# The recurrent branch of a fused two-block kernel: decay bias added on VectorE, decay and gate products interleaved, both running sums in one product

## The chip, the cores and the metric

The kernel runs as one program on one core of a Trainium2 chip. The time is the device time of one execution in microseconds (us), and the kernel before took 2842.14 us (median of three runs, 2840.62 to 2842.34). The engines are called by the profile's short names: PE (TensorE matmul), PEld (its weight loads), DVE (VectorE), ACT (ScalarE), POOL (GpSimd) and SP (SyncE, which issues the weight transfers).

## The reference, cut to what matters

The whole program is a first block (spatial gating, dilated attention, two mixtures of experts) followed by a second block of two layers. Each of these two layers is a feed-forward part, a mixer of three branches (retention, sparse attention, recurrence), and another feed-forward part. The change is in the recurrent branch alone, so it runs twice in an execution.

```python
def rwkv7_time_mix(p, mu, w0, w2, a0, a2, g2, k_k, k_a, r_k, ln_w, ln_b):
    r, k, v, w_lr, a_lr, g_lr = split_cols(token_shift(p, mu), RWKV_SIZES)
    log_decay = -jax.nn.softplus(-(w0 + jnp.tanh(w_lr) @ w2).astype(f32)) - 0.5
    decay = jnp.exp(-jnp.exp(log_decay))
    a = jax.nn.sigmoid((a0 + a_lr @ a2).astype(f32))
    g = jax.nn.sigmoid(g_lr) @ g2
    kk = heads(k * k_k)
    kk = kk / jnp.maximum(jnp.sqrt(jnp.sum(kk * kk, axis=-1, keepdims=True)), 1e-12)
    k_h = heads(k) * (1.0 + (a_h - 1.0) * k_a...)
    ...  # a scan over 256 tokens with decay, k_h, kk and a; then a group norm and the gate g
```

Here exp(log_decay) is exp(-0.5) times sigmoid(w0 + tanh(w_lr) w2). The kernel does the scan in chunks of 64 tokens, and needs for that the running sum of this sigmoid over the tokens of a chunk, once with the token itself (inclusive) and once without it (strict), and exponentials of both.

## The kernel before, in words

There are 256 tokens, held as two tiles of 128 (`T` = 2), and 512 channels of the branch, held as four tiles of 128. Every engine has its own program, and all meet at numbered pieces of PSUM: piece n lies in bank n modulo 4 (`BANKS`). PE fills a piece (`pe.take()`, wait on `s_free`, then the products with `s_full` at the end), and the engine that reads it frees the bank (`s_free`). Each engine's program counts every piece, and passes with `skip` over those that are others' work. So PE can't start piece n before piece n - 4 has been read, and the engine that reads a piece does it when its own program gets there. There is no planner; the order is as written, on each engine.

Around the change, PE's order in `pe_rwkv` (line 2845) is this:

- the channel products of the branch (`pe_chan`), then `pe_merge_sparse(0)`: a gate product and a product of the sparse branch, one piece each
- `pe_headsum_of_tokens(TMP)`: eight products with two output columns each, one piece. DVE reads it in `v_rates_of_tokens` (lines 2828 to 2834)
- for each token tile, the decay product (`LORA[0:64]` with the upper 64 rows of `LR`) and a product with one row, ones times `W0R`, that adds the bias w0 in the same piece (lines 2876 and 2877)
- four products of `LORA[64:128]` for a, two pieces (line 2882), and four of `G2` for the gate g, two pieces (line 2889)
- the running sums: `LWT` times the table `cumulate`, whose first 128 columns make the strict and the other 128 the inclusive sum; the inclusive ones first (`m` = 1), two pieces each, 16 products in all (line 2902)
- `pe_to_heads(RSS)`: 32 small products that spread the reciprocal norms of kk over the channels, two pieces, then `pe_merge_sparse(1)` and so on.

ACT reads the decay pieces with a sigmoid (line 3068), the a pieces with a sigmoid and the bias a0 (3073), copies the g pieces (3079), takes the square root of the head norms (line 827, in `s_root`), and then does the exponentials of the sums (3084, 3085, 3089). The square root and the exponential each need a load of ACT's function table. DVE, after `v_merge_sparse(0)`, makes the low part of a split weight block (`v_ahead(34)`, line 2038), which waits for ACT's high part of the same block (`s_ahead(34)`, line 2030), which waits for the block's transfer; then comes `v_rates_of_tokens` (line 2832), and the next thing is the reciprocal of the roots (2838). Block 34 is one of the weight blocks that SP loads into a ring of five slots. `s_params` (line 2305) issues the transfers of the branch's small weights, w0's at line 2310, at the start of the layer's mixer.

## Time and profile before

| | |
|---|---|
| device time, median of three runs | 2842.14 us (2840.62 to 2842.34) |
| span of the profiled execution, first to last instruction | 2833.1 us |
| PE busy | 2648.3 us (93%) |
| DVE busy | 1269.9 us (45%) |
| ACT busy | 838.0 us (30%) |
| mean granted clock of TensorE, as a share of full speed | 0.980 |
| this stretch in layer 1 of the second block | about 1656 to 1684 us |
| this stretch in layer 2 | about 2454 to 2481 us |

The profile gives one execution by its span, 2833.1 us. A run's time also holds what lies ahead of the first instruction and behind the last one: 9.0 us against the median. A busy share of 93% for PE is an average over the whole program. What a change in one stretch is worth must be read in the stretch: which engine is waited for there, and how fast TensorE's clock runs in it.

### The profile page before, as it was taken

To read this page: it belongs to the slowest core of one execution; us is meant where nothing else is said; L and a number is where in the kernel's file an instruction comes from. 1 tells how busy PE (TensorE), PEld (TensorE's weight loads), DVE (VectorE), ACT (ScalarE), POOL (GpSimd) and SP (SyncE) were. 2 spreads that over 40 slices of the span, in tenths; PEclk is the share of its full clock that TensorE was granted. 3 is DMA by queue.
4 is the path that set the end of the run, shared out by engine and by line. 5 is a ranking of instruction groups with operands and counts; after the bars stand their busy time and mean duration, and the time that the engine had idled before them with its cause. 6 is when DMAs were issued, how large, how long until landed. Compare 5 with 4: busy or idle time off the path is not lost.

```text
span 2833.1 us, 46156 instructions
## 1 busy us (share of the span) xinstructions
PE 2648.3 (93%) x19543; PEld 2036.8 (72%) x19543; DVE 1269.9 (45%) x1869; ACT 838.0 (30%) x1039; POOL 0.2 (0%) x4
## 2 busy tenths in 40 slices
PE   8899888879899888879999999999999999999998
PEld 8743433348543333369999889999899998899998
DVE  5610110046411000055657756655655667666555
ACT  4300000025210000033343432443433444423433
POOL 0000000000000000000000000000000000000000
PEclk9999999999999999999999999999999999999999
DMA  8689999972799999955563431445555544323553
GB/s 269 256 358 425 426 425 426 425 267 90 311 401 425 425 425 425 426 170 182 196 218 122 133 119 62 135 164 179 179 179 190 186 152 134 105 76 102 167 179 134
DMA packets 286235, 684.65 MB, mean 242 GB/s; under 512 B 11962, under 2 KB 217586, under 8 KB 236660
## 3 DMA queue, kind: packets, MB, share of 16 engines
q1 hardware_dynamic: 282792, 671.27, 63.2%
q10 hardware_dynamic: 3276, 10.93, 1.0%
q8 instruction: 132, 2.16, 0.3%
q14 instruction: 35, 0.29, 0.0%
HBM read 681.11 MB, written 1.05 MB: 241 GB/s over the span
## 4 chain that ended last, share of the span: by engine, by line
PE 71%; DMA 20%; DVE 5%; ACT 2%; issue 1%; DVEq 1%; SPq 0%; ACTq 0%; POOLq 0%
PE psum L419 69%; DMA weight_ring<-in_w_gate 14%; DMA weight_ring<-in_w_up 3%; DMA weight_ring<-in_w_down 2%; PE psum L427 1%; DVE weight_ring_parts L2038 1%; ACT weight_ring_parts L2030 1%; DVEq L552 1%; DVE arena L3230 0%; DMA h_tok<-in_mem 0%; SPq L1893 0%; DVE arena L3256 0%; DVE arena L1809 0%; DMA weight_ring<-in_w_in 0%; DVE arena_parts L2127 0%
## 5 line engine op out<-in xcount | busy, mean ns | idle before, releaser
L419 PE MATMUL psum<-weight_ring_parts,arena_parts 128*128 128x256 f32 (+1 forms) x2992 | 671.5, 317 | 4.9 <-DVE arena_parts L2131 1.9
L2038 DVE TENSOR_TENSOR weight_ring_parts<-weight_ring,weight_ring_parts 128x2048 fp32r<-128x2048 f32 x217 | 496.6, 2291 | 347.1 <-ACT weight_ring_parts L2030 341.1
L419 PE MATMUL psum<-x_chan_parts,weight_ring_parts 128*128 128x256 f32 x3200 | 611.5, 282 | 13.1 <-DVE arena_parts L2127 7.9
L2030 ACT ACTIVATE weight_ring_parts<-weight_ring 128x2048 fp32r<-128x2048 f32 x217 | 414.9, 1913 | 483.3 <-POOLq L532 347.4
L419 PE MATMUL psum<-weight_ring,arena 128*64 128x512 f32 (+1 forms) x2112 | 474.8, 582 | 73.5 <-DMA weight_ring<-in_w_gate 38.9
L419 PEld LDWEIGHTS psum<-weight_ring_parts,arena_parts 128*128 128x128 f32 x2992 | 501.5, 191 | 41.4 <-DVE arena_parts L2131 2.1
L419 PEld LDWEIGHTS psum<-x_chan_parts,weight_ring_parts 128*128 128x128 f32 x3200 | 508.5, 190 | 18.5 <-issue 13.2
L419 PE MATMUL psum<-arena 64*64 64x64 f32 (+7 forms) x4616 | 492.6, 335 | 29.5 <-DVE arena L1809 15.8
L419 PEld LDWEIGHTS psum<-weight_ring,arena 128*64 128x64 f32 (+1 forms) x2112 | 179.3, 140 | 361.1 <-issue 358.2
L419 PEld LDWEIGHTS psum<-arena 64*64 64x64 f32 (+3 forms) x4616 | 261.3, 141 | 237.3 <-issue 210.9
L419 PE MATMUL psum<-weight_ring_parts,x_chan_parts 128*128 128x256 f32 x2336 | 427.8, 285 | 1.6 <-DVE arena_parts L2127 1.6
L419 PE MATMUL psum<-arena_parts,weight_ring_parts 128*128 128x256 f32 x1536 | 419.2, 283 | 0.0
L419 PEld LDWEIGHTS psum<-weight_ring_parts,x_chan_parts 128*128 128x128 f32 x2336 | 360.8, 190 | 9.2 <-issue 7.5
L419 PEld LDWEIGHTS psum<-arena_parts,weight_ring_parts 128*128 128x128 f32 x1536 | 285.2, 190 | 1.3
L1825 DVE TENSOR_TENSOR arena<-arena,psum 128x512 f32<-128x512 f32 x32 | 22.0, 688 | 520.8 <-PE psum L419 519.5
L1809 DVE COPY arena<-psum 128x512 f32<-128x512 f32 x48 | 33.2, 692 | 296.8 <-PE psum L419 262.4
L1671 ACT ACTIVATE arena<-psum 128x512 f32<-128x512 f32 x32 | 19.1, 597 | 484.4 <-PE psum L419 484.4
L1664 ACT ACTIVATE arena<-psum 128x512 f32<-128x512 f32 (+1 forms) x80 | 34.3, 467 | 371.3 <-PE psum L419 334.5
L2038 DVE TENSOR_TENSOR weight_ring_parts<-weight_ring,h_tok_parts 128x2048 fp32r<-128x2048 f32 x32 | 73.3, 2292 | 64.7 <-ACT h_tok_parts L2030 63.9
L419 PE MATMUL psum<-arena_parts,h_tok_parts 128*128 128x256 f32 x320 | 90.0, 281 | 0.0
L419 PE MATMUL psum<-x_chan_parts,h_tok_parts 128*128 128x256 f32 x320 | 89.6, 280 | 0.0
L2030 ACT ACTIVATE h_tok_parts<-weight_ring 128x2048 fp32r<-128x2048 f32 x32 | 61.1, 1911 | 71.5 <-POOLq L532 34.2
(322 smaller groups left out, 1742.9 us busy)
## 6 DMA issues: line engine op xcount, KB each, us to landing
weight_ring<-in_w_gate SPq DMA_DIRECT2D x92, 1024.0 KB, 23.2
weight_ring<-in_w_up SPq DMA_DIRECT2D x92, 1024.0 KB, 22.9
weight_ring<-in_w_in SPq DMA_DIRECT2D x70, 1024.0 KB, 5.2
arena<-in_w_down SPq DMA_DIRECT2D x64, 1024.0 KB, 22.5
weight_ring<-in_w_down SPq DMA_DIRECT2D x64, 1024.0 KB, 23.2
weight_ring<-in_ffa_w_in SPq DMA_DIRECT2D x44, 1024.0 KB, 7.2
weight_ring<-in_ffb_w_in SPq DMA_DIRECT2D x44, 1024.0 KB, 5.6
arena<-in_w_gate SPq DMA_DIRECT2D x36, 1024.0 KB, 18.5
```

The lines of the kernel that those rows point to most:

```text
L419: return nc.tensor.matmul(*args, **kw)
L427: last = nc.tensor.transpose(ps[0:cols, b, lo:lo + rows], src, ident[0:rows, 0:rows])
L552: self.e.drain()
L1664: nc.scalar.activation(dst, ps[:, b, 0:dst.shape[1]], ACT.Copy).then_inc(s_free[b], 1)
L1671: nc.scalar.activation(SILU[:, half, :], ps[:, b, :], ACT.Silu).then_inc(s_free[b], 1)
L1809: nc.vector.tensor_copy(dst, ps[:, b, :]).then_inc(s_free[b], 1)
L1825: nc.vector.tensor_tensor(HG[:, half * 512:(half + 1) * 512], SILU[:, half, :], ps[:, b, :], ALU.mult).then_inc(s_free[b], 1)
L2030: nc.scalar.activation(HIGH[buf], ring[:, sl, :], ACT.Copy).then_inc(s_hi, 1)
L2038: nc.vector.tensor_tensor(ring_parts[:, sl, :], ring[:, sl, :], f32(HIGH[buf]), ALU.subtract).then_inc(s_split, 1)
```

## The change

There are three edits, and one that follows from them.

1. The bias w0 is no longer a product. It is loaded as 128 equal rows (`W0B`) where it was one row (`W0R`), DVE adds it to the decay piece on the way into `LWT` in SBUF, and ACT takes the sigmoid there, in place, once DVE has signalled it.
2. The decay product of a token tile, which uses the upper 64 rows of the array, is followed at once by two of the four products of a, which use the lower 64 rows.
3. The strict and the inclusive sum of a channel and token tile are one product with 256 moving columns. A piece then holds both sums of one channel tile, so that ACT takes its exponentials per channel tile, 256 elements each.
4. PE waits for two signals from ACT ahead of the running sums, where it waited for the two banks to be read. The square root needs no wait of its own.

```diff
-        W0R = sb("decay_bias_row", [1, 512])
+        W0B = sb("decay_bias_rows", [P, 512])
...
-            s.e.dma_start(W0R[0:1, :], a["rwkv_w0_2"][bass.ds(l, 1), :]).then_inc(s_load["w0"], 16)
+            s.e.dma_start(W0B[:, :], a["rwkv_w0_2"][l].partition_broadcast(P)).then_inc(s_load["w0"], 16)
...
-                pe.mm(ps[:, b, :], LR[0:64, 0, t * P:(t + 1) * P], LORA[0:64, :], start=True, stop=False)
-                pe.mm(ps[:, b, :], ones2[0:1, :], W0R[0:1, :], start=False, stop=True).then_inc(s_full[b], 1)
-            for c in range(0, 4, 2):
+                pe.mm(ps[:, b, :], LR[0:64, 0, t * P:(t + 1) * P], LORA[0:64, :], start=True, stop=True).then_inc(s_full[b], 1)
                 b = pe.take()
                 pe.e.wait_ge(s_free[b], pe.emptied())
                 for j in range(2):
-                    last = pe.mm(ps[:, b, j * SEQ:(j + 1) * SEQ], LORA[64:128, (c + j) * P:(c + j + 1) * P],
+                    c = 2 * t + j
+                    last = pe.mm(ps[:, b, j * SEQ:(j + 1) * SEQ], LORA[64:128, c * P:(c + 1) * P],
                                  LR[64:128, 0, :], start=True, stop=True)
...
-            for m in (1, 0):
-                for c in range(0, 4, 2):
-                    b = pe.take()
-                    pe.e.wait_ge(s_free[b], pe.emptied())
-                    for j in range(2):
-                        for t in range(T):
-                            last = pe.mm(ps[:, b, j * SEQ + t * P:j * SEQ + (t + 1) * P],
-                                         LWT[:, t, (c + j) * P:(c + j + 1) * P], cumulate[:, m * P:(m + 1) * P],
-                                         start=True, stop=True)
-                    last.then_inc(s_full[b], 1)
+            pe.e.wait_ge(s_a2p, pe.c["a2p"].next(T))
+            for c in range(4):
+                b = pe.take()
+                pe.e.wait_ge(s_free[b], pe.emptied())
+                for t in range(T):
+                    last = pe.mm(ps[:, b, t * 2 * P:(t + 1) * 2 * P], LWT[:, t, c * P:(c + 1) * P], cumulate,
+                                 start=True, stop=True)
+                last.then_inc(s_full[b], 1)
...
             for t in range(T):
-                b = s.take()
-                s.e.wait_ge(s_full[b], s.filled())
-                nc.scalar.activation(LWT[:, t, :], ps[:, b, :], ACT.Sigmoid).then_inc(s_free[b], 1)
-            for c in range(0, 4, 2):
+                s.skip()
+
+                s.e.wait_ge(s_v2a, s.c["v2a"].next(2 if t == 0 else 1))
+                nc.scalar.activation(LWT[:, t, :], LWT[:, t, :], ACT.Sigmoid).then_inc(s_a2p, 1)
...
-            s_root(RSS[:, :, :])
+            nc.scalar.activation(RSS[:, :, :], RSS[:, :, :], ACT.Sqrt).then_inc(s_a2v, 1)
...
+            for c in range(4):
                 b = s.take()
                 s.e.wait_ge(s_full[b], s.filled())
+                sums = ps[:, b, :].rearrange("p (t m n) -> p m t n", t=T, m=2)
+                nc.scalar.activation(by_token_tile(PI, c), sums[:, 1], ACT.Exp, scale=-DECAY)
+                nc.scalar.activation(by_token_tile(IPI, c), sums[:, 1], ACT.Exp, scale=DECAY)
+                nc.scalar.activation(by_token_tile(PEX, c), sums[:, 0], ACT.Exp, scale=-DECAY).then_inc(s_free[b], 1)
...
             v_rates_of_tokens(1.0, 1e-24, ALU.mult, ALU.max)
-            rates = v.pieces.n + 2
-            v.skip(10)
+            v.e.wait_ge(s_load["w0"], v.c["l_w0"].next())
+            rates = v.pieces.n + 1
+            for t in range(T):
+                b = v.take()
+                v.e.wait_ge(s_full[b], v.filled())
+                nc.vector.tensor_tensor(LWT[:, t, :], ps[:, b, :], W0B[:, :], ALU.add).then_inc(s_free[b], 1)
+                v.sync()
+                nc.vector.nop().then_inc(s_v2a, 1)
+                v.skip()
+            v.skip(6)
```

On PE, behind the products of the head norms (`tables,arena 128x2`), the difference reads as follows. `norm_gain_bias` holds `LORA` and `G2`, `decay_bias_row` is `W0R`, and `piece_free2_two` is the bank of the head norms.

```order
 L419 MATMUL psum<-tables,arena 128x2 x7
-L419 MATMUL psum<-norm_gain_bias,arena 128x512 [waits scalar_to_tensor_two,piece_free3_two,loaded_w0,loaded_lora]
-L419 MATMUL psum<-decay_bias_row,tables 128x512
-L419 MATMUL psum<-norm_gain_bias,arena 128x512 [waits piece_free0_two]
-L419 MATMUL psum<-decay_bias_row,tables 128x512
-L419 MATMUL psum<-arena,norm_gain_bias 128x256 [waits piece_free1_two]
+L419 MATMUL psum<-norm_gain_bias,arena 128x512 [waits piece_free3_two,scalar_to_tensor_two,loaded_lora]
+L419 MATMUL psum<-arena,norm_gain_bias 128x256 [waits piece_free0_two]
 L419 MATMUL psum<-arena,norm_gain_bias 128x256
+L419 MATMUL psum<-norm_gain_bias,arena 128x512 [waits piece_free1_two]
 L419 MATMUL psum<-arena,norm_gain_bias 128x256 [waits piece_free2_two]
 L419 MATMUL psum<-arena,norm_gain_bias 128x256
```

The two one-row products are gone, the second decay product stands behind the first two products of a, and the wait for bank 2 stays where it was, with the third product of a, now with two products fewer ahead of it.

On ACT, at the same place, before:

```order
L2030 ACTIVATE weight_ring_parts<-weight_ring 128x2048 [waits slots_used_two,slot_loaded4_two]
L3068 ACTIVATE arena<-psum 128x512 [waits piece_full3_two]
L3068 ACTIVATE arena<-psum 128x512 [waits piece_full0_two]
L3073 ACTIVATE arena<-psum,small 128x256 [waits piece_full1_two]
L3073 ACTIVATE arena<-psum,small 128x256
L3073 ACTIVATE arena<-psum,small 128x256 [waits piece_full2_two]
L3073 ACTIVATE arena<-psum,small 128x256
L3079 ACTIVATE arena<-psum 128x512 [waits piece_full3_two]
L3079 ACTIVATE arena<-psum 128x512 [waits piece_full0_two]
L827 ACT_TABLE_LOAD
L827 ACTIVATE small<-small 128x16 [waits vector_to_scalar_two]
L3084 ACT_TABLE_LOAD
```

and ACT now, where line 3062 is the decay's sigmoid, 3067 that of a, 3073 the copy of g, 3074 the root, and 3083 the first exponential:

```order
L2030 ACTIVATE weight_ring_parts<-weight_ring 128x2048 [waits slots_used_two,slot_loaded4_two]
L3062 ACTIVATE arena<-arena 128x512 [waits vector_to_scalar_two]
L3067 ACTIVATE arena<-psum,small 128x256 [waits piece_full0_two]
L3067 ACTIVATE arena<-psum,small 128x256
L3062 ACTIVATE arena<-arena 128x512 [waits vector_to_scalar_two]
L3067 ACTIVATE arena<-psum,small 128x256 [waits piece_full2_two]
L3067 ACTIVATE arena<-psum,small 128x256
L3073 ACTIVATE arena<-psum 128x512 [waits piece_full3_two]
L3073 ACTIVATE arena<-psum 128x512 [waits piece_full0_two]
L3074 ACT_TABLE_LOAD
L3074 ACTIVATE small<-small 128x16
L3083 ACT_TABLE_LOAD
```

Both decay sigmoids now wait for DVE and not for PE, and the second stands between the two pairs for a; the copies, the root and the two table loads keep their order.

## Rows read from the trace of the kernel before

**Rows 1.** The page: its first line, and GB/s moved in 40 equal slices of the span.
```profile
span 2833.1 us, 46156 instructions
...
GB/s 269 256 358 425 426 425 426 425 267 90 311 401 425 425 425 425 426 170 182 196 218 122 133 119 62 135 164 179 179 179 190 186 152 134 105 76 102 167 179 134
```

**Rows 2.** Chain that ended last, 1640 to 1740: start us, length us, what.
```profile
1680.95 31.41 PE psum L419 x228
```

**Rows 3.** Timeline, layer 1: start us, length us, engine, line, what [idle before <-releaser].
```profile
1656.85 3.62 PE L419 MATMUL psum<-weight_ring,arena 128*128 128x256 f32 x16
...
1660.50 0.69 DVE L2387 TENSOR_TENSOR arena<-arena,psum 128x512 f32<-128x512 f32 x1 [2.56 <-PE psum L419]
...
1662.07 1.12 PE L419 MATMUL psum<-norm_gain_bias,arena 64*128 64x512 f32 x2
...
1663.12 1.71 PE L419 MATMUL psum<-decay_bias_row,tables 1*128 1x512 f32 x2
1663.46 1.91 ACT L2030 ACTIVATE weight_ring_parts<-weight_ring 128x2048 fp32r<-128x2048 f32 x1 [5.82 <-DMA weight_ring<-in_w_in]
...
1664.76 2.07 PE L419 MATMUL psum<-norm_gain_bias,arena 64*128 64x512 f32 x2
...
1665.40 2.29 DVE L2038 TENSOR_TENSOR weight_ring_parts<-weight_ring,weight_ring_parts 128x2048 fp32r<-128x2048 f32 x1 [3.43 <-ACT weight_ring_parts L2030]
...
1666.76 2.07 PE L419 MATMUL psum<-decay_bias_row,tables 1*128 1x512 f32 x2
1667.61 0.17 DVE L2832 TENSOR_SCALAR small<-psum 128x16 f32<-128x16 f32 x1
...
1668.76 7.49 PE L419 MATMUL psum<-arena,norm_gain_bias 64*128 64x256 f32 x16
...
1670.87 0.84 ACT L3073 ACTIVATE arena<-psum,small 128x256 f32<-128x256 f32 x2 [1.41 <-PE psum L419]
1672.47 3.06 PEld L419 LDWEIGHTS psum<-arena,norm_gain_bias 128*128 128x128 f32 x8 [0.65 <-issue]
...
1676.04 4.29 PE L419 MATMUL psum<-tables,arena 128*128 128x128 f32 x32
1676.29 0.60 ACT L3079 ACTIVATE arena<-psum 128x512 f32<-128x512 f32 x1 [1.11 <-PE psum L419]
...
1679.72 0.60 ACT L3084 ACTIVATE arena<-psum 128x512 f32<-128x512 f32 x1
...
1680.22 0.59 ACT L3085 ACTIVATE arena<-psum 128x512 f32<-128x512 f32 x1
...
1680.95 1.98 PE L419 MATMUL psum<-tables,small 128*64 128x128 f32 x32 [0.62 <-ACT arena L3085]
...
1682.86 0.50 PE L419 MATMUL psum<-weight_ring_parts,x_chan_parts 128*128 128x256 f32 x2
```

**Rows 4.** Timeline, layer 2, the same stretch.
```profile
2464.66 0.17 DVE L2832 TENSOR_SCALAR small<-psum 128x16 f32<-128x16 f32 x1
...
2472.96 3.73 PE L419 MATMUL psum<-tables,arena 128*128 128x128 f32 x32
...
2476.60 0.60 ACT L3084 ACTIVATE arena<-psum 128x512 f32<-128x512 f32 x1
...
2479.74 0.51 PE L419 MATMUL psum<-weight_ring_parts,x_chan_parts 128*128 128x256 f32 x2
```

**Rows 5.** Busy time by stretch; PEclk, after the engines, is the granted clock.
```profile
1663.00:1664.00 1.00, 1.00 (x3) 0.29 (x2) 0.00 (x0) 0.54 (x1) 0.00 (x0) 0.76 0.00 0
...
1676.00:1678.00 2.00, 2.00 (x14) 1.96 (x13) 0.00 (x0) 1.70 (x2) 0.00 (x0) 0.70 0.00 0
...
2476.00:2478.00 2.00, 0.87 (x11) 0.70 (x11) 1.93 (x4) 1.99 (x4) 0.00 (x0) 1.00 0.00 0
```

**Rows 6.** The instructions of line 3073: duration ns min/median/max, first and last start.
```profile
L3073 ACT ACTIVATE arena<-psum,small x8: 466/470/473, 1670.9 to 2470.3; 128x256 f32<-128x256 f32 x8
```

**Rows 7.** DMA issues: queue, count, KB each, median us to landing.
```profile
norm_gain_bias<-in_rwkv_g ACTq DMA_DIRECT2D x2, 256.0 KB, 9.1
```

More of the change, by code:

```diff
@@ L2869, in pe_rwkv @@
             pe.e.wait_ge(s_load["lora"], pe.c["l_lora"].next(3))
-            pe.e.wait_ge(s_load["w0"], pe.c["l_w0"].next())
             pe.e.wait_ge(s_a2p, pe.c["a2p"].next())
@@ L2891, in pe_rwkv @@
                 last.then_inc(s_full[b], 1)
-            pe.e.wait_ge(s_free[(pe.pieces.n - 6) % BANKS], pe.read_out(pe.pieces.n - 6))
-            pe.e.wait_ge(s_free[(pe.pieces.n - 5) % BANKS], pe.read_out(pe.pieces.n - 5))
-            for m in (1, 0):
-                for c in range(0, 4, 2):
-                    b = pe.take()
-                    pe.e.wait_ge(s_free[b], pe.emptied())
-                    for j in range(2):
-                        for t in range(T):
-                            last = pe.mm(ps[:, b, j * SEQ + t * P:j * SEQ + (t + 1) * P],
-                                         LWT[:, t, (c + j) * P:(c + j + 1) * P], cumulate[:, m * P:(m + 1) * P],
-                                         start=True, stop=True)
-                    last.then_inc(s_full[b], 1)
+            pe.e.wait_ge(s_a2p, pe.c["a2p"].next(T))
[6 more added lines that the diff above has]
+                last.then_inc(s_full[b], 1)
             pe_to_heads(RSS)
@@ L3072, in s_rwkv @@
                 for j in range(2):
-                    last = nc.scalar.activation(WA[:, c + j, :], ps[:, b, j * SEQ:(j + 1) * SEQ], ACT.Sigmoid,
-                                                bias=pv("rwkv_a0")[:, c + j:c + j + 1])
+                    c = 2 * t + j
+                    last = nc.scalar.activation(WA[:, c, :], ps[:, b, j * SEQ:(j + 1) * SEQ], ACT.Sigmoid,
+                                                bias=pv("rwkv_a0")[:, c:c + 1])
                 last.then_inc(s_free[b], 1)
@@ L3079, in s_rwkv, with by_token_tile @@
                 nc.scalar.activation(flat(WG[:, c:c + 2, :]), ps[:, b, :], ACT.Copy).then_inc(s_free[b], 1)
-            s_root(RSS[:, :, :])
-            for c in range(0, 4, 2):
+            nc.scalar.activation(RSS[:, :, :], RSS[:, :, :], ACT.Sqrt).then_inc(s_a2v, 1)
+            def by_token_tile(x, c):
+                return x[:, c, :].rearrange("p (t n) -> p t n", t=T)
+            for c in range(4):
                 b = s.take()
                 s.e.wait_ge(s_full[b], s.filled())
-                nc.scalar.activation(flat(PI[:, c:c + 2, :]), ps[:, b, :], ACT.Exp, scale=-DECAY)
-                nc.scalar.activation(flat(IPI[:, c:c + 2, :]), ps[:, b, :], ACT.Exp, scale=DECAY).then_inc(s_free[b], 1)
-            for c in range(0, 4, 2):
-                b = s.take()
-                s.e.wait_ge(s_full[b], s.filled())
-                nc.scalar.activation(flat(PEX[:, c:c + 2, :]), ps[:, b, :], ACT.Exp, scale=-DECAY).then_inc(s_free[b], 1)
+                sums = ps[:, b, :].rearrange("p (t m n) -> p m t n", t=T, m=2)
+                nc.scalar.activation(by_token_tile(PI, c), sums[:, 1], ACT.Exp, scale=-DECAY)
+                nc.scalar.activation(by_token_tile(IPI, c), sums[:, 1], ACT.Exp, scale=DECAY)
+                nc.scalar.activation(by_token_tile(PEX, c), sums[:, 0], ACT.Exp, scale=-DECAY).then_inc(s_free[b], 1)
             s.skip(2)
@@ L3171, in v_rwkv @@
             v_rates_of_tokens(1.0, 1e-24, ALU.mult, ALU.max)
-            rates = v.pieces.n + 2
-            v.skip(10)
+            v.e.wait_ge(s_load["w0"], v.c["l_w0"].next())
[8 more added lines that the diff above has]
+            v.skip(6)
             v_reciprocal_of_rates()
-            for n in (rates, rates + 1):
+            for n in (rates, rates + 2):
                 v.e.wait_ge(s_free[n % BANKS], v.read_out(n))
```

## Prediction

> **What bounds the kernel now.** I started with the page. The span is 2833.1 us [rows 1] and PE is busy for 93% of it, which says only that PE is usually the bound. Then I read the chain that ended last, in order of time, around this stretch of layer 1. It has one unbroken piece of PE from 1680.95 on, 31.41 us long [rows 2], and the pieces just before it are on ACT. The timeline shows why. PE does the running sums from 1676.04, but what comes next, the spreading of the norms at 1680.95, waits 0.62 us for ACT's exponential of line 3085, which frees its bank [rows 3]. ACT is late since its work is serial behind PE: the last copy of g starts at 1676.29, 0.25 us behind PE's last gate product (PE's next work starts at 1676.04), and then come the copy (0.60), two table loads and the root, so that the first exponential starts at 1679.72. So 3.43 us lie between the start of the last copy and the first exponential, and 3.68 between the end of PE's gate products and it. In layer 2 the same distance is 2476.60 - 2472.96 = 3.64 [rows 4].
>
> What the reader is to see: in this stretch the end is set by PE's products up to the last gate product, plus ACT's fixed 3.7 us, and not by the running sums. And PE's products are dear here. The first decay product took 1.05 us to the next start (1662.07 to 1663.12), the second 2.00 (1664.76 to 1666.76) [rows 3]. The windows say why: the granted clock averages 0.76 in 1663 to 1664, so it falls to its lower level of 1.2 GHz about half way, and averages 0.70 in 1676 to 1678, so it comes back about 1677.2 [rows 5]. Four gate products at the low level took 1676.04 - 1672.47 = 3.57 us (0.89 each), four products of a 1672.47 - 1668.76 = 3.71 (0.93 each); at full clock eight products of 256 columns (16 records, two for each) took 3.62 us, 0.45 each at most [rows 3].
>
> There is a third chain, hidden now. DVE reads the head norms only at 1667.61, behind the low part of weight block 34 at 1665.40, behind ACT's high part at 1663.46, which waited for the block's transfer [rows 3]. Call the end of that read V: 1667.61 + 0.17 = 1667.78 in layer 1, and 2464.66 + 0.17 = 2464.83 in layer 2 [rows 3, 4]. It frees bank 2, for which the third product of a waits. Before, PE reached that product about 1668.76 + 1.86 = 1670.6, 2.8 us later than V, so nobody waited.
>
> **The change part by part.** The time is the span plus 9.0 us for what lies around it (2842.14 - 2833.1), and I take the change of the span as the change of the time.
>
> *Bias products removed.* From start to next start they took 1.64 us (1663.12 to 1664.76) and 2.00 us (1666.76 to 1668.76), so 3.64 in layer 1 [rows 3]. Taken alone that would be the gain, and some 7 us in both layers. It can't all arrive: PE now runs into the wait for V.
>
> *Decay and a in alternating halves.* The first decay product, two of a, and the second decay product need between 1.9 us (if the halves run beside each other) and 3.0 us (2 x 1.05 and 2 x 0.45, one after the other at full clock). PE starts them at 1662.07 and is through by 1665.1 at the latest at full clock, and by about 1666.5 if the clock falls at 1663.5 as before. V is at 1667.78. So whatever the halves give, PE then idles for 1.3 to 3.8 us. I cost the interleaving at zero: its cover is the wait for V. If block 34 were early, it would be worth up to 1.1 us a layer.
>
> *PE behind V.* I take the low clock, since it had fallen before with PE busy and now PE idles as well. Two products of a cost 1.86, four gate products 3.57 (their banks are freed by DVE's first add at about V + 0.8 and by ACT's first pair at about V + 2.3, both earlier than PE needs them). With 0.05 to start, PE is through at V + 5.48: 1673.26 in layer 1, where it was 1676.04, and 2470.31 in layer 2, where it was 2472.96. So -2.78 and -2.65.
>
> *ACT and the DVE adds.* Each add is a 128x512 DVE operation from PSUM like the one at 1660.50, 0.69 us [rows 3]; with hand-over about 0.1. The first sigmoid of the decay can start at V + 0.9, the second at V + 2.2. With 0.5 to 0.6 for each (the copy of 512 elements took 0.60), and 0.84 or less for each pair of a (the row at 1670.87), ACT is through with a at V + 3.5 to V + 3.8, while PE's first gate piece is ready at about V + 3.7 and its second at V + 5.5. At the low clock ACT waits for PE, and the sigmoids cost nothing. At full clock they would be the bound, see the rivals.
>
> *Fixed tail.* Copy, two table loads and root are unchanged: first exponential at PE's end + 3.68. So 1676.94 and 2473.95 (with 3.64).
>
> *Running sums.* Eight products of 256 columns where there were 16 of 128, the same columns. Bounds: 3.6 us at full clock (8 x 0.45), 7.1 at the low one (8 x 0.89). From V + 5.5 they end between V + 9.1 and V + 12.6. The first bank is released by the exponentials at V + 10.5. So they are covered if the clock comes back within some 4 us of their start. It came back 4.7 us behind the start of the gate products in layer 1 (1672.47 to 1677.2), hence I take V + 6.7 and the sums end near V + 9.7: covered.
>
> *Narrower exponentials.* This speaks against the change. Those of 512 elements follow each other at 0.50 us (1679.72 to 1680.22); two of 256 took 0.84 together [rows 3] with 0.47 for one [rows 6], so they follow at 0.37. Twelve cost 11 x 0.37 + 0.47 = 4.5 us where six cost 5 x 0.50 + 0.60 = 3.1. What counts is when PE can go on. The merge product needed the bank freed by the fifth one, and before it started 1682.86 - 1679.72 = 3.14 behind the first exponential, being held up by the spreading products. Now it needs the ninth: 8 x 0.37 + 0.47 + 0.14 = 3.57. That is +0.43 a layer. Bounds: 0 (spreading alone decides) and +0.85 (spacing 0.42).
> The Trainium skill, page "VectorE: DVE Perf Modes", section on the TRN2 errata, says that an ACT or DVE operation pays a fixed cost per instruction, so that many small tiles pay it many times, and gives ScalarE 172 cycles plus one per element for PSUM sources. By that estimate twelve narrow ones cost 12 x 0.36 = 4.3 us and six wide ones 6 x 0.57 = 3.4, a rise of 0.9 where the rows give 1.4. The rows decide, and the sum stands.
>
> *The wider transfer.* w0 is now 256 KB where it was 2 KB, the size of g2's block, which lands in 9.1 us [rows 7]. It is issued at the start of the mixer and needed only behind V, after the retention and the sparse branch. It could hold up the weight blocks beside it by its own length, between 0 and 0.6 us (254 KB at the page's highest rate of 426 GB/s [rows 1]); I take 0, since only the queue's order is changed and the blocks are loaded ahead of their use.
>
> *Sum.* -2.78 + 0.43 = -2.35 in layer 1, -2.65 + 0.43 = -2.22 in layer 2, together -4.6 us. Behind 1682.86 PE is dense for 30 us [rows 2], and the loads that feed it are released by PE itself, so the gain should reach the end. 2842.14 - 4.6 = 2837.5, a span of about 2828.5.
>
> **The rivals.**
>
> *A. ACT bound, full clock: more gain.* If TensorE's clock is back while PE does a and g, ACT's own row from V is the bound: first decay sigmoid V + 0.9, 0.5, pair 0.74, 0.5, pair 0.74, copies 0.50 + 0.60, so V + 4.5, and 2.83 for tables and root: first exponential at V + 7.3. That is 1675.1 and 2472.1, or -4.6 and -4.5; less 0.43 each, -8.2 in all: 2833.9. For it: bias and half-empty products, which stood in the stretch where the clock fell, are fewer. Against: PE idles ahead of V. A mixture, the clock returning during the gate products, lies between.
>
> *B. Running sums are the bound: the gain nearly vanishes.* If the clock stays low until they are done (V + 12.6), spreading starts at V + 12.6 where it was V + 13.2, and itself takes 1.9 to 3.8. Between -0.6 and +1.3 a layer: about 2842.5, and 2840.5 if one layer only is so. Against: the clock came back 4.7 us into such products.
>
> *C. Slower: the clock falls a second time.* The change leaves PE idle for about 0.8 us (V + 9.7 to V + 10.5) ahead of the 32 small spreading products. If the clock then falls and stays low into the merge products, each us of it costs up to half. It decides against the change beyond some 4.6 us low in each layer. A low stretch as long as before (1663.5 to 1677.2, 13.7 us) would cost 6.8 a layer, 13.7 - 4.6 = +9.1: 2851; a short one of 6 us in each layer 6 - 4.6 = +1.4: 2843.6. Against: in layer 2 PE was busy for 0.87 of 2 us in 2476 to 2478 at a clock of 1.00, and full clock went on [rows 5].
> The Trainium skill, page "TensorE: Matmul & The Clock Gate", names gaps between bursts of products as what sends the clock back to half; by it both the wait for V and this gap are a risk, while the rows show one such gap without a fall.
>
> *D. The transfer of w0 delays the entry of the layer.* At most 0.6 each, +1.2 on the forecast: 2838.7.
>
> **How the numbers follow.** Forecast, including the clock returning a little earlier during the gate products (up to 1 us a layer more): 0.56. A: 0.12. B: 0.18. C: 0.07. D: 0.07. A measurement of this kernel tells 0.2%, or 5.7 us, from no change, so the line lies at 2836.5. Faster gets A and a third of the forecast's share: 0.30. Slower by over 0.2% (2847.8) is only the long form of C: 0.05; the rest, 0.65, is within. The range goes from A's time to just above B's: 2833.9 to 2842.3.
>
> **What would show it.** Right: DVE's read of the head norms stays near 1667.6, the first exponential of layer 1 at about 1677, the merge product at about 1680.5; PE idle ahead of the third product of a with DVE line 2832 as what it waited for; the releaser of the spreading products is ACT's third exponential; the clock low from the decay products to the first running sums. Wrong: if the first exponential lies before 1676, the clock was back (A); if PE is busy right up to the spreading products, the sums were the bound (B); a clock below 1.00 in the merge products is C. The forecast fails as a whole if block 34 lands at another time, as V is the origin of everything.

## The result, and the profile after

The changed kernel took 2830.40 us (median of 20 runs, 2824.58 to 2839.78). The kernel before, run beside it, took 2838.03 (20 runs, 2830.68 to 2842.34). The ratio is 0.9978, 95% interval 0.9969 to 0.9987, which on 2838.03 is -6.2 us (-8.8 to -3.7); the quotient of the two medians, 0.9973, lies in that interval. So the change makes the kernel faster by about 0.2%. The forecast of -4.6 us lies in that interval. The forecast time, 2837.5, doesn't fit, and 2830.4 lies below the range that ended at 2833.9.

The profiled execution of the changed kernel has this span:

```profile
span 2836.5 us, 46096 instructions
```

Its time was 2838.36 us, near the upper end of its 20 runs, and only 1.9 us lie around its span. It can't be set against the span of before, 2833.1 [rows 1], to read the gain: these two executions differ by more than the change. Between 2540 and 2610 us, in code that the change doesn't touch, the two compare as follows, first before, then after (columns as in [rows 5], the clock is the third number from the end):

```profile
2540.00:2610.00 70.00, 68.13 (x1140) 63.91 (x1136) 42.45 (x63) 22.45 (x28) 0.00 (x0) 1.00 0.23 78
```

```profile
2540.00:2610.00 70.00, 68.43 (x947) 63.94 (x943) 35.53 (x54) 20.19 (x22) 0.00 (x0) 0.85 0.23 73
```

TensorE is busy alike, at a clock of 0.85 where it was 1.00. By an estimate from these rows that alone costs about 70 x 0.15 = 10 us. It isn't the change's doing: in the second profile of the changed kernel (see the last experiment) the same stretch has a clock of 1.00. The runs differ in the same way: of the changed kernel's, the shortest had a mean clock of 0.985 (2824.58 us) and the longest 0.976 (2839.78). I therefore compare the changed stretch by its own length, from the first two-column product of the head norms to the first product of the following merge, and the whole by runs.

The chain that ended last, in layer 1, after the change (start us, length us, what):

```profile
1658.35 6.37 DMA weight_ring<-in_w_in
...
1664.75 1.92 ACT weight_ring_parts L2030
...
1666.69 2.29 DVE weight_ring_parts L2038
...
1669.12 5.80 PE psum L419 x12
...
1674.94 0.60 ACT arena L3073
...
1675.55 1.28 ACT L3074
...
1678.38 0.38 ACT arena L3083
...
1679.46 20.70 PE psum L419 x157
```

Ahead of the products of a, the chain now goes through weight block 34: its transfer, ACT's high part, DVE's low part. That chain was hidden before, behind the bias products. The timeline of layer 1 after, which answers to [rows 3]:

```profile
1661.56 1.84 PE L419 MATMUL psum<-tables,arena 128*128 128x2 f32 x16
...
1663.33 0.69 PE L419 MATMUL psum<-norm_gain_bias,arena 64*128 64x512 f32 x1
1663.34 0.70 PE L419 MATMUL psum<-arena,norm_gain_bias 64*128 64x256 f32 x2
...
1664.30 1.02 PE L419 MATMUL psum<-norm_gain_bias,arena 64*128 64x512 f32 x2
...
1668.90 0.17 DVE L2832 TENSOR_SCALAR small<-psum 128x16 f32<-128x16 f32 x1
1669.12 5.78 PE L419 MATMUL psum<-arena,norm_gain_bias 64*128 64x256 f32 x12 [3.80 <-DVE small L2832]
...
1674.69 4.11 PE L419 MATMUL psum<-tables,arena 128*128 128x256 f32 x16
...
1678.38 0.38 ACT L3083 ACTIVATE arena<-psum 128x256 f32<-128x256 f32 x1
...
1678.66 0.38 ACT L3084 ACTIVATE arena<-psum 128x256 f32<-128x256 f32 x1
1678.92 0.39 ACT L3085 ACTIVATE arena<-psum 128x256 f32<-128x256 f32 x1
...
1679.46 1.97 PE L419 MATMUL psum<-tables,small 128*64 128x128 f32 x32 [0.65 <-ACT arena L3085]
...
1681.35 0.50 PE L419 MATMUL psum<-weight_ring_parts,x_chan_parts 128*128 128x256 f32 x2
```

PE is through with its first work at 1665.3 and idles 3.80 us until DVE has read the head norms (V, 1669.07). The sums start at 1674.69 = V + 5.62, the first exponential 3.69 later, and the merge product 2.97 behind that. In layer 2 the wait is 2.58 us:

```profile
2463.48 4.70 PE L419 MATMUL psum<-arena,norm_gain_bias 64*128 64x256 f32 x12 [2.58 <-DVE small L2832]
```

The clock in layer 1 after, which answers to [rows 5], and the last three rows are in layer 2:

```profile
1664.00:1666.00 2.00, 1.31 (x7) 0.25 (x3) 0.00 (x0) 1.25 (x1) 0.00 (x0) 1.00 0.01 3
1666.00:1668.00 2.00, 0.00 (x0) 0.00 (x0) 1.31 (x1) 0.66 (x1) 0.00 (x0) 1.00 0.00 0
1668.00:1670.00 2.00, 0.88 (x2) 0.79 (x3) 1.76 (x3) 0.00 (x0) 0.00 (x0) 0.71 0.00 0
1670.00:1672.00 2.00, 2.00 (x5) 1.17 (x5) 0.69 (x1) 1.95 (x5) 0.00 (x0) 0.50 0.00 0
...
1674.00:1676.00 2.00, 2.00 (x7) 1.61 (x6) 0.00 (x0) 1.04 (x2) 0.00 (x0) 0.58 0.00 0
1676.00:1678.00 2.00, 2.00 (x11) 1.74 (x11) 0.90 (x4) 1.97 (x3) 0.00 (x0) 1.00 0.00 0
1678.00:1680.00 2.00, 1.35 (x14) 0.95 (x14) 1.84 (x4) 1.99 (x8) 0.00 (x0) 1.00 0.00 0
...
2462.00:2464.00 2.00, 0.52 (x2) 0.48 (x3) 1.80 (x3) 0.00 (x0) 0.00 (x0) 1.00 0.00 0
2464.00:2466.00 2.00, 2.00 (x6) 1.16 (x5) 1.01 (x2) 1.60 (x4) 0.00 (x0) 0.54 0.00 0
2466.00:2468.00 2.00, 2.00 (x7) 1.60 (x6) 0.00 (x0) 1.56 (x4) 0.00 (x0) 0.61 0.00 0
```

Before, TensorE's clock fell at about 1663.5, with PE busy on decay and bias products. After, in layer 1, it stays at full through these products and through two microseconds without any, and falls at about 1668.8, near the end of the idle time. In layer 2 it is still at full when PE goes on at 2463.48, and falls at about 2464.2, so the fall comes with the wait for V, but not always inside it. It is at 1.2 GHz for about 7 us in layer 1 (before: 13.7) and 3.4 in layer 2 (before: 10.2), from windows of 1 us.

The stage in us from its start, layer 1 / layer 2, in all kernels whose cause is argued below ("late" is block 34's split moved behind the exponentials, see the experiments):

| kernel | V | sums start | first exponential | merge product | change of both stages |
|---|---|---|---|---|---|
| before | 7.48 / 6.53 | 15.74 / 14.66 | 19.42 / 18.30 | 22.56 / 21.44 | |
| changed | 7.51 / 6.28 | 13.13 / 10.86 | 16.82 / 14.50 | 19.79 / 17.48 | -6.7 |
| changed, second profile | 7.42 / 6.33 | 12.95 / 10.61 | 16.63 / 14.29 | 19.61 / 17.26 | -7.1 |
| bias on VectorE only | 7.62 / 6.47 | 13.25 / 11.05 | 16.93 / 14.69 | 20.07 / 17.84 | -6.1 |
| no alternation | 7.58 / 6.00 | 13.20 / 10.20 | 16.88 / 13.88 | 19.86 / 16.86 | -7.3 |
| sums joined only | 7.60 / 6.16 | 14.66 / 14.63 | 18.30 / 18.27 | 21.28 / 21.25 | -1.5 |
| before, late | 2.05 / 2.05 | 14.67 / 15.40 | 18.30 / 19.08 | 21.45 / 22.22 | -0.3 |
| the same, bias full height | 2.05 / 2.05 | 15.72 / 15.37 | 19.40 / 19.06 | 22.54 / 22.20 | +0.7 |
| the same, bias behind a | 2.04 / 2.05 | 7.44 / 7.45 | 11.59 / 11.60 | 14.73 / 14.74 | -14.5 |
| the same, no bias | 2.05 / 2.05 | 5.54 / 5.54 | 9.66 / 9.66 | 12.80 / 12.80 | -18.4 |
| changed, late | 2.05 / 2.05 | 6.16 / 6.15 | 10.20 / 10.19 | 13.17 / 13.17 | -17.7 |
| changed, late, no alternation | 2.05 / 2.05 | 6.11 / 6.10 | 10.51 / 10.50 | 13.49 / 13.48 | -17.0 |
| changed, late, g copied by VectorE | 2.05 / 2.05 | 6.15 / 6.15 | 9.22 / 9.22 | 12.20 / 12.20 | -19.6 |

### The profile page after: what moved, and what is told of

Its sections match the earlier page's. It is cut to its first block, busy times and chain, and to the rows that moved or that the text cites. A ratio compares the mean times of both kernels' runs of the same rounds, so it can differ in the third digit from the quotient of the medians.

```text
span 2836.5 us, 46096 instructions
## 1 busy us (share of the span) xinstructions
PE 2646.5 (93%) x19503; PEld 2041.3 (72%) x19503; DVE 1272.4 (45%) x1873; ACT 838.5 (30%) x1051; POOL 0.2 (0%) x4
## 3 DMA queue, kind: packets, MB, share of 16 engines
HBM read 681.63 MB, written 1.05 MB: 241 GB/s over the span
## 4 chain that ended last, share of the span: by engine, by line
PE 70%; DMA 20%; DVE 5%; ACT 2%; issue 1%; DVEq 1%; SPq 0%; ACTq 0%; POOLq 0%
PE psum L419 69%; DMA weight_ring<-in_w_gate 14%; DMA weight_ring<-in_w_up 3%; DMA weight_ring<-in_w_down 2%; DVE weight_ring_parts L2038 1%; PE psum L427 1%; ACT weight_ring_parts L2030 1%; DVEq L552 1%; DMA weight_ring<-in_w_in 0%; DVE arena L3234 0%; DMA weight_ring<-in_w_in_a 0%; DMA h_tok<-in_mem 0%; SPq L1893 0%; DVE arena L3260 0%; PE psum L686 0%
```

## The experiments

**Is the wait for V the new bound?** Block 34's split (`s_ahead(34)` and `v_ahead(34)`) moves from ahead of the decay work to behind the exponentials; nothing else of the changed kernel does.

```diff
             s_merge_sparse(0)
-            s_ahead(34)
...
             s.skip(2)
+            s_ahead(34)
             s_merge_sparse(1)
...
             v_merge_sparse(0)
-            v_ahead(34)
             v_rates_of_tokens(1.0, 1e-24, ALU.mult, ALU.max)
...
+            v_ahead(34)
             v_merge_sparse(1)
```

> The changed kernel, with the split of weight block 34 moved on ACT and DVE from ahead of the head norms' read to behind the exponentials, so that V (the end of DVE's read of the head norms) no longer waits for that block's transfer. Stage length = from the start of PE's head-norm products (128x2) to the start of the first product of the next merge; it was 22.6 and 21.4 us before and is 19.8 and 17.5 in the changed kernel. Theory (V is the bound behind the change): V falls to about 0.3 us behind the head-norm products, PE does not wait ahead of the third product of a, the bound becomes ACT's own row (V + 7.3 to the first exponential, 3.0 more to the merge), stage length 12.5 to 15 us in both layers, 5 to 12 us less in all than the changed kernel, ratio to before 0.993 to 0.996. Rival (the gain came from fewer product columns at the low clock, V is only a bystander): stage length falls by under 1 us against the changed kernel, ratio 0.998. Rival 2: the gain is given back in the later merge, whose product waits for block 34's low part: PE idle there by the 4 us that were saved.

Measured: 2819.07 us (6 runs), ratio 0.9930 (0.9914 to 0.9945) to the kernel before at 2836.98, that is -19.9 us; the two stages are 17.7 shorter. PE no longer waits for V, and the clock stays at full:

```profile
1662.16 0.59 PE L419 MATMUL psum<-norm_gain_bias,arena 64*128 64x512 f32 x1
1662.17 1.70 PE L419 MATMUL psum<-arena,norm_gain_bias 64*128 64x256 f32 x6
1664.18 1.13 PE L419 MATMUL psum<-arena,norm_gain_bias 128*128 128x256 f32 x4 [0.31 <-ACT arena L3066]
1665.15 3.62 PE L419 MATMUL psum<-tables,arena 128*128 128x256 f32 x16
1670.27 1.97 PE L419 MATMUL psum<-tables,small 128*64 128x128 f32 x32 [1.50 <-ACT arena L3084]
```

```profile
1659.00:1672.00 13.00, 11.19 (x85) 9.34 (x83) 6.86 (x12) 9.17 (x22) 0.00 (x0) 1.00 0.09 29
```

The wait for V was the bound in the changed kernel, and the clock fell with it: without the wait it doesn't fall. With it gone ACT's row is the bound: PE waits for ACT's exponentials for 1.50 us.

**Is the late block alone worth it?** The same move in the kernel before.

> The kernel before with only block 34's split moved behind the exponentials. Theory: before the change PE reached the third product of a 2.8 us behind V in layer 1, so V was not the bound there: stage length stays at 22.6 and 21.4 us within 1 us, ratio 1.000 (0.999 to 1.001). Rival (the block was the bound all along and the change itself did little): stage length falls by 2 us or more, ratio 0.998 or less.

Measured: 2837.68 us (12 runs), ratio 0.9996 (0.9980 to 1.0012); the stages change by -1.1 and +0.8. Nothing, since PE never waited for V there. The -17.7 are a joint effect: the change brings the wait for V into the open, and only then is moving block 34 worth something. The timeline of this kernel shows the dear products still there, with V already past:

```profile
1662.63 1.12 PE L419 MATMUL psum<-norm_gain_bias,arena 64*128 64x512 f32 x2
1663.69 1.12 PE L419 MATMUL psum<-decay_bias_row,tables 1*128 1x512 f32 x2
1664.74 1.79 PE L419 MATMUL psum<-norm_gain_bias,arena 64*128 64x512 f32 x2
1666.46 2.07 PE L419 MATMUL psum<-decay_bias_row,tables 1*128 1x512 f32 x2
1668.45 3.78 PE L419 MATMUL psum<-arena,norm_gain_bias 64*128 64x256 f32 x8
```

**What is the alternation worth?** The changed kernel with both decay products ahead of the four products of a (on all engines), first as it is, then with block 34 late.

```diff
             for t in range(T):
                 b = pe.take()
                 pe.e.wait_ge(s_free[b], pe.emptied())
                 pe.mm(ps[:, b, :], LR[0:64, 0, t * P:(t + 1) * P], LORA[0:64, :], ...)
+            for t in range(T):
                 b = pe.take()
```

> The changed kernel with only the alternation undone: both decay products, then the four products of a; the rest as changed. Theory: V covers it, stage length as in the changed kernel, 19.8 and 17.5 us within the 1.5 us that the clock's return can move it, PE idle ahead of the third product of a 0.9 us shorter, ratio to before 0.998. Rival (alternation is what made the gain or held the clock): stage length 21 us or more, clock low for 10 us or more in the stretch as before.

> As the kernel with block 34 late, but both decay products first and then the four products of a (one half of the array after the other). Here the wait for V no longer covers it. Theory (interleaving was worth nothing in the change because V covered it): now PE needs up to 0.9 us more for the six products at full clock, but ACT is the bound, so the stage is 0 to 0.9 us longer per layer than with alternation. Rival (the halves beside each other are what keeps the clock up): the granted clock falls to its low level in this stretch and the stage is 2 us or more longer.

Measured: 2825.90 us (7 runs), ratio 0.9963 (0.9949 to 0.9977), and late 2817.62 (6 runs), 0.9930 (0.9913 to 0.9947). The first is no slower than the changed kernel, its stages are even 0.6 us shorter, little more than the 0.4 by which the changed kernel's two profiles differ. I had expected PE's idle time ahead of the third product of a to be 0.9 us shorter, and it wasn't: 3.88 us where it was 3.80, behind 1.99 us of work in either order. With block 34 late the alternation is worth 0.3 us a layer, and that on ACT's side, since PE starts the sums at 6.11 without and 6.16 with it. The reason is in the timeline without alternation. Its program has decay, decay, a, a, a, a, each float32 product recorded as two:

```profile
1662.94 0.69 PE L419 MATMUL psum<-norm_gain_bias,arena 64*128 64x512 f32 x1
1662.96 0.70 PE L419 MATMUL psum<-arena,norm_gain_bias 64*128 64x256 f32 x2
1663.48 0.59 PE L419 MATMUL psum<-norm_gain_bias,arena 64*128 64x512 f32 x1
1663.49 0.59 PE L419 MATMUL psum<-arena,norm_gain_bias 64*128 64x256 f32 x2
1663.90 0.59 PE L419 MATMUL psum<-norm_gain_bias,arena 64*128 64x512 f32 x1
```

The first products of a start 0.02 us behind the first decay product and ahead of the second: two halves of the array run side by side although the program doesn't alternate.

**The bias on VectorE alone, and the joined sums alone.** The first has the new adds with the old order and the old 16 sums, the second the kernel before with only the 8 wide sums and the 12 narrow exponentials.

> The kernel before with edit 1 alone: w0 is added by DVE and the sigmoid is taken in place; both decay products come first, then the four of a; the running sums are 16 products of 128 columns and six exponentials of 512 elements, as before. Stage length (start of the 128x2 head-norm products to the first product of the next merge) was 22.6 and 21.4 us before and 19.8 and 17.5 in the changed kernel. Theory (edit 1 carries the gain, down to the wait for V): 20.0 us in layer 1 and 17 to 18.5 in layer 2, the changed kernel's plus 0.2 for the tail, ratio 0.998 (0.997 to 0.999). Rival (alternation and the joined sums carry it): 21.5 us or more, ratio 0.9995 or above.

> The kernel before with edit 3 alone: both running sums in one product of 256 columns, one piece per channel tile, twelve exponentials of 256 elements. Theory (the sums are covered by ACT's table loads; narrow exponentials follow each other at 0.265 us, so that the tail from the first exponential to the merge is 2.97 us where it was 3.14): stage 22.4 and 21.3 us, ratio 0.9995 to 1.000, no measurable change. Rival (my forecast's term: narrow exponentials cost 0.43 us a layer): 23.0 and 21.9 us. Rival (the joined sums are a part of the gain): 21.5 us or less.

Measured: bias alone 2828.06 us (12 runs), ratio 0.9970 (0.9956 to 0.9983) to the kernel before at 2835.34, stages -6.1; sums alone 2840.43 (12 runs), ratio 1.0011 (0.9996 to 1.0026), stages -1.5, which the time doesn't confirm. So the bias carries the change. In the sums-only kernel the clock still falls about 4 us into the stage. Its layer 1 took 21.28 us, below the 21.5 that I had named as the sign that the joined sums are a part of the gain. But 1.1 us of it lie ahead of the sums (their start at 14.66 where it was 15.74), where this kernel is the kernel before: the clock fell 4.0 us into the stage and not 3.2. From the first exponential on it has the 2.98 us expected.

**Why does the clock fall?** My idea after these was that a one-row product leaves the array nearly empty. So, in the kernel before with block 34 late, the bias became a product with all 128 rows.

```diff
-                pe.mm(ps[:, b, :], ones2[0:1, :], W0R[0:1, :], start=False, stop=True)
+                pe.mm(ps[:, b, :], ident, W0B[:, :], start=False, stop=True)
```

> The kernel before with block 34's split late, and the bias product with all 128 rows: the identity times 128 equal rows of w0, where it was one row of ones times one row of w0. The same columns and the same order of products; no add on DVE. The granted clock fell inside the stage before (low for 13.7 and 10.2 us) and stays at full in the kernels without the one-row product and without a wait for V. Theory (the clock falls in this stretch because of what the one-row products leave idle in the array): clock at 1.00 through the stage or low for under 4 us, PE through with the gate products some 7 us behind the start of the decay products where it was 12.9, stage 16 us or less, ratio 0.995 or less. Rival (the clock falls because of the products with two columns and the half-height ones, whatever the bias product is): low for 7 us or more and stage above 19 us, ratio 0.999 or more.

Measured: 2832.38 us (12 runs), ratio 0.9987 (0.9970 to 1.0004), stages +0.7: no difference that these runs can tell. The idea fell, the clock drops with full-height bias products too, 3.3 and 3.6 us into the stage, where it was 4.2 and 3.6 with the one-row ones:

```profile
1662.00:1664.00 2.00, 2.00 (x3) 0.52 (x3) 0.00 (x0) 0.56 (x1) 0.00 (x0) 0.54 0.00 0
```

Next, from the same kernel (before, late), once without the bias products (w0 isn't added), and once with the same one-row products issued behind the products of a, where they add to the same pieces.

```diff
-                pe.mm(ps[:, b, :], ones2[0:1, :], W0R[0:1, :], start=False, stop=True).then_inc(s_full[b], 1)
...
                 last.then_inc(s_full[b], 1)
+            for b in decays:
+                pe.mm(ps[:, b, :], ones2[0:1, :], W0R[0:1, :], start=False, stop=True).then_inc(s_full[b], 1)
             for c in range(0, 4, 2):
```

> The kernel before with block 34's split late and the two one-row bias products left out (w0 isn't added at all). Theory 1, the bias products are what lets the clock fall: the clock stays at 1.00 as in the late-block version of the changed kernel, and the running sums start near 6.2 us behind the start of the head norms, where they started at 14.7 with the bias products; merge product near 13.4 (13.17 + 0.2 for the wider exponentials and the sums' two products each). Theory 2, the clock falls for another reason (the old order of decays and a, or the sixteen products of the sums): it falls near +4 and the sums start no earlier than +8.5, the merge product at 15.5 or later.

> The kernel before with block 34's split late and the two one-row bias products moved behind the four products of a. Theory 1a, what matters is that decays and a stand next to each other and so run side by side in two halves: they do so here, and the clock stays at 1.00 at least up to the bias products; gate products start near +6.3 (3.9 for decays and a at the earliest seen, 1.9 for the bias), sums near +8.1 where they started at 14.7. Theory 1b, the one-row products themselves let the clock fall wherever they stand: it falls within 2 us behind them, so the gate products take 0.9 us each, and the sums start at +9.5 or later.

Measured in one run each, too few to compare times by: 2815.09 us without the bias, 2819.31 with it behind a. What follows rests on the two stages of each run's profile, which agree within 0.01 us. Both kernels start the sums 0.7 us earlier than I had worked out. The second is the telling one, since it does every product of the kernel before (timeline, then clock):

```profile
1658.87 0.69 PE L419 MATMUL psum<-norm_gain_bias,arena 64*128 64x512 f32 x1
1658.88 0.70 PE L419 MATMUL psum<-arena,norm_gain_bias 64*128 64x256 f32 x2
...
1660.80 1.98 PE L419 MATMUL psum<-decay_bias_row,tables 1*128 1x512 f32 x4
1662.71 1.99 PE L419 MATMUL psum<-arena,norm_gain_bias 128*128 128x256 f32 x8
1664.54 3.73 PE L419 MATMUL psum<-tables,arena 128*128 128x128 f32 x32
```

```profile
1657.00:1661.00 4.00, 4.00 (x31) 3.49 (x30) 1.55 (x3) 0.00 (x0) 0.00 (x0) 1.00 0.36 120
1661.00:1663.00 2.00, 2.00 (x5) 0.75 (x5) 0.00 (x0) 0.78 (x2) 0.00 (x0) 1.00 0.00 0
```

Decays and a take 1.93 us together (1658.87 to 1660.80), the two bias products 1.91, and the clock stays at 1.00, in the windows shown and on to 1672. The stage is 6.7 and 7.5 us shorter than with the bias between (21.45 and 22.22 to 14.73 and 14.74), by order alone. Leaving the products out gives another 1.93 a layer (12.80). So what the bias products themselves cost is the smaller part; what they did by standing between the halves, to the overlap and to the clock, is three to four times that. An estimate from rows parts the two: at full clock the old order would take four products of 1.05 and four of 0.45, 6.0 us, where the new one takes 1.93 + 1.91 = 3.8. So about 2.2 us are lost overlap. The sums start 7.2 us (layer 1) and 8.0 us (layer 2) earlier, so 5 to 6 are the clock's.

**Who is the bound once V is gone?** The changed kernel, late, with the two copies of g on VectorE.

```diff
-                nc.scalar.activation(flat(WG[:, c:c + 2, :]), ps[:, b, :], ACT.Copy).then_inc(s_free[b], 1)
...
+                nc.vector.tensor_copy(flat(WG[:, c:c + 2, :]), ps[:, b, :]).then_inc(s_free[b], 1)
```

> The changed kernel with block 34's split late, and the two copies of the gate g made by DVE in place of ACT. Theory (with V gone, ACT's serial row is the bound, and these copies are 1.1 us of it): the first exponential comes 1.0 us earlier, stage 12.2 us in both layers where it is 13.2 with block 34 late alone, ratio to before 0.9925. Rival (PE's running sums, which end 9.8 us into the stage, or the DVE adds are the bound by then): stage falls by less than 0.4 us.

Measured: 2813.41 us (6 runs), ratio 0.9920 (0.9902 to 0.9938), -22.7 us on 2835.34. The first exponential comes 0.98 us earlier, the merge product 0.97, the length of two copies less their hand-over. This version beats both kernels.

**Does the gain repeat?** The changed kernel again, five runs beside nine of before.

> The changed kernel once more, beside the two below. If its gain over the kernel before is real and the same, the ratio is again near 0.998 (an interval that holds 0.9984, which is -4.6 us, and 0.9976, which is the 6.7 us read from the stage in the first profile). A second profile should show the stage within 0.3 us of the first: merge product 19.8 us behind the start of the head norms in layer 1 and 17.5 in layer 2, V at 7.5 and 6.3.

Measured: 2829.07 us (2825.81 to 2833.18), ratio 0.9957 (0.9943 to 0.9970) to 2841.74. Its stages agree with the first profile within 0.3 us (table), as expected. The ratio doesn't: I had expected an interval that holds 0.9984 and 0.9976, and this one holds neither. -12.2 us is more than the 7.1 of the stages, and the interval ends at -8.5. The medians of before over the four comparisons were 2838.03, 2836.98, 2835.34 and 2841.74, so the base moves by 6.4 us between them, while the changed kernel gave 2830.40 and 2829.07. The sign is sure, the stage accounts for about 7 us, and whether the rest is more than this moving base stays open.

## Why the prediction was right or wrong

**The base of the time: wrong, and the first cause of the miss.** The failed step is "2842.14 - 4.6 = 2837.5, a span of about 2828.5", with "9.0 us" for what lies around the span. The profiled execution wasn't one of the three runs. All whose span is known show 1.8 to 1.9 us around the span, so the page's execution had a time near 2835 and wasn't like the three, which turned out to be among the highest of 20 (median 2838.03, highest 2842.34). With the base right the same sum gives 2833.4. A range from 2833.9 to 2842.3 was the width of the mechanisms alone; the runs of one kernel spread by 12 to 15 us, and the base of three of them deserved some 5 us of its own.

**The sum: mechanism right, size 2.2 us too small.** It said -4.6 (-2.35 in layer 1, -2.22 in layer 2), the stages gave -6.7 (-2.77 and -3.96). Base (-4.1) and sum (-2.2) bring 2837.5 to 2831.2, and the last 0.8 lies within the interval. Term by term:

- *PE behind V*: right. It idles ahead of the third product of a in both layers, released by DVE's line 2832, for 3.80 and 2.58 us where I had 1.3 to 3.8. Forecast V + 5.48 for the start of the sums; 5.62 in layer 1.
- *Layer 2*: there the clock fell only 0.7 us behind PE's new start and came back during the gate products (0.54 in 2464 to 2466, 0.61 in 2466 to 2468), so the sums start at V + 4.58. That is worth 0.9 us, and I had it in the text as a mixture with A, not in the sum. V itself came 0.25 earlier in the stage.
- *Narrower exponentials*: mis-sized. "With 0.47 for one, so they follow at 0.37", +0.43 a layer. They start every 0.265 us (1678.38 to 1681.30 in eleven steps), twelve cost 11 x 0.265 + 0.50 = 3.4 where the six wide ones cost 3.1, and the merge product comes 2.97 behind the first where it came 3.14. So -0.17, and not +0.43: 1.2 us over both layers. The path was wrong too: I let the merge product wait for the ninth exponential, which was over at 1680.98, 0.37 us ahead of it. What sets its start is the spreading products, as in my lower bound. They start 1.08 us behind the first exponential, released by the third narrow one, where it was 1.23, released by the second wide one, and take 1.9 as before. My row was the sigmoid of a, whose bias is a value per partition; the exponentials have a constant scale and no such operand. The trace of before has the difference in other lines: the copies of 256 elements from PSUM in line 670, without such an operand, took 382 ns, the sigmoids of a 470. That the operand and not the function makes it wasn't tested by itself, but a row with the same operands was there to be read. The Trainium skill, page "ScalarE: Activation LUTs", section "What ACT_TABLE_LOAD costs", says that each operand of one value per partition adds about 93 ns. By that estimate 0.37 becomes 0.28, and the measured 0.265 comes near it. The 0.36 that I had weighed, from the Trainium skill's page "VectorE: DVE Perf Modes", section on the TRN2 errata, is near the 0.38 that the first exponential took, and not near the distance at which they follow each other.
- *Interleaving at zero*: right in the sum, since it is covered by the wait for V, and the version without it is no slower. But its value without that cover, "up to 1.1 us a layer", was too high: 0.3, as the halves overlap in either order.
- *Fixed tail* of 3.68: 3.69 and 3.64. *Running sums covered*: yes, PE waited 0.65 and 1.10 us for ACT behind them. *The wider transfer*: no sign of it; V is 7.51 us into layer 1's stage where it was 7.48, and from w0's issue (line 2310) to the stage there are 240.3 and 242.5 us in the two layers, where there were 241.2 and 241.6.

**What I read wrongly in a right sum.** I took the low clock for granted "since it had fallen before with PE busy". The place where the removed products stood was the reason for that early fall: in all four kernels with bias products between decay and a, in both layers, the clock falls 3.2 to 4.2 us into the stage, and in none of the others before 7.0. The changed kernel's clock fell at another place, with the wait for V. In layer 1 the sum came out nearly right all the same: PE had nothing to do in the time at full clock that I had not foreseen, and the clock fell just as PE went on. That was luck; in layer 2, and in layer 1 of the second profile, it fell behind PE's new start.

**The rivals.** A (ACT bound at full clock, -8.2) didn't happen as the change was made, but is the state of the kernel once block 34 is late: first exponential at V + 8.1 there, of which V + 4.1 is PE's start of the sums. B (sums the bound) is refuted by PE's wait for ACT. C (the clock falls again ahead of the spreading products) is refuted: 1.00 from 1676 on, in spite of 0.65 us idle. D would show in that distance from w0's issue to the stage: in the second profile it is 240.1 and 241.1 us, shorter than before in both layers.

## What to carry to other kernels

Count what an instruction does to its neighbours: a cheap product between two that could share the array can cost several times its own length (here 1.9 us by itself and 6.7 to 7.5 by where it stood), and moving it may bring most of what removing it does. When a removal exposes another chain (here a weight split ahead of a small read), look at once for what can be moved behind it; the second edit was worth more than the first and nothing without it. Size a small operation from a row with the same operands, and give the base of a forecast its own spread.

## What the runs showed that I had not expected

- Products on one half of the array started beside and ahead of earlier ones on the other half (a at 1662.96 with the second decay product, its records from 1663.90 on, still to come). Two decay and four a products took 1.93 us side by side, where one decay product alone took 1.06.
- A full-height bias product takes as long as a one-row one, 2.07 us for both its records at the low clock in either kernel. What in the order decay, bias, decay, bias lets the clock fall isn't settled (it falls 1.5 to 2.4 us behind the first decay product, with PE busy): neither the empty rows (full height falls too) nor the products as such (behind a they don't) do. That they keep the halves from overlapping is what all these kernels have in common; it was not isolated further.
- The clock stayed at full in a window of two microseconds without a product (1666 to 1668), and fell only near the end of the idle time of 3.80 us, in layer 2 (2.58 us idle) even 0.7 us behind it. So the price was paid by the products that followed: 0.9 us for each of 256 columns, until about 1675.7. Idle times of 0.3 to 1.8 us in the late kernels brought no fall.
